# A chunked recurrence on TensorE: chunk matrices in 128x128 blocks, or as 64 columns with 64x64 quarter tiles

## What is computed

```python
def step(S, inp):
    r_t, w_t, k_t, v_t, kk_t, a_t = inp
    s_kk = jnp.einsum('bhvk,bhk->bhv', S, kk_t)
    S = (S * w_t[:, :, None, :] - s_kk[..., None] * (kk_t * a_t)[:, :, None, :]
         + v_t[..., None] * k_t[:, :, None, :])
    return S, jnp.einsum('bhvk,bhk->bhv', S, r_t)
...
_, y = lax.scan(step, S0, xs)
```

## Time and profile before

| | |
|---|---|
| device time, median of 3 runs | 1858.79 us (1856.99 to 1859.38) |
| profiled execution | its span, 1854.8 us, first to last instruction; the page gives no other time of its own |
| PE busy | 1814.8 us, 98% |
| PEld busy | 1670.1 us, 90% |
| DVE busy | 1234.7 us, 67% |
| ACT busy | 822.3 us, 44% |
| HBM traffic | 389.6 MB, 210 GB/s over the span |

### The profile page before, as it was taken

One profiled execution on the slowest core, in us unless ns is written; L12 is line 12 of the kernel. 1 busy time (PEld: TensorE's weight loads), 2 busy tenths in 40 slices (PEclk: granted clock), 3 DMA queues, 4 the chain that ended last, 5 costly groups with the idle time before them and its releaser, 6 DMA issues.

```text
span 1854.8 us, 30243 instructions
## 1 busy us (share of the span) xinstructions
PE 1814.8 (98%) x12578; PEld 1670.1 (90%) x12578; DVE 1234.7 (67%) x1826; ACT 822.3 (44%) x1106; POOL 0.2 (0%) x4
## 2 busy tenths in 40 slices
PE   9999999899999999999999999999999999999999
PEld 8889888788887779999978899999999997889999
DVE  3894455777888787876657468776876547555543
ACT  2335443543676674434443244344534444334442
POOL 0000000000000000000000000000000000000000
PEclk9999999999999999999999999999999999999999
DMA  8334310888798886786430058775785341044451
GB/s 320 136 137 159 137 69 25 329 316 305 302 359 329 337 343 256 310 332 255 165 111 24 23 217 341 301 323 229 293 320 226 159 159 46 4 157 157 164 202 69
DMA packets 65224, 391.62 MB, mean 211 GB/s; under 512 B 7360, under 2 KB 7488, under 8 KB 27328
## 3 DMA queue, kind: packets, MB, share of 16 engines
q1 hardware_dynamic: 64800, 389.61, 54.3%
q10 hardware_dynamic: 288, 0.08, 0.0%
HBM read 388.61 MB, written 1.05 MB: 210 GB/s over the span
## 4 chain that ended last, share of the span: by engine, by line
PE 88%; DVE 8%; ACT 2%; issue 1%; DVEq 0%; ACTq 0%
PE bank L501 87%; DVE region L2213 1%; PE bank L542 1%; DVE slab_low L1892 1%; DVE region L2176 0%; DVE region L1905 0%; DVE tiny L2175 0%; DVE region L2501 0%; DVE region L2478 0%; DVE region L2499 0%; DVE region L2167 0%; DVE slab_low L1973 0%; ACT region L1398 0%; DVE region L2497 0%; ACT L1328 0%
## 5 line engine op out<-in xcount | busy, mean ns | idle before, releaser
L1892 DVE TENSOR_TENSOR slab_low<-slab,w_hi 128x2048 fp32r<-128x2048 f32 x152 | 346.0, 2289 | 96.1 <-ACT w_hi L1441 95.4
L501 PE MATMUL bank<-h_hi,w_hi 128*128 128x256 f32 x1408 | 392.4, 282 | 0.0
L501 PE MATMUL bank<-h_hi,slab_low 128*128 128x256 f32 x1408 | 391.8, 281 | 0.0
L501 PE MATMUL bank<-h_lo,w_hi 128*128 128x256 f32 x1408 | 381.0, 282 | 0.0
L1441 ACT ACTIVATE w_hi<-slab 128x2048 fp32r<-128x2048 f32 x152 | 291.3, 1918 | 78.1 <-DMA slab<-in_w_ffn_in 66.6
L501 PEld LDWEIGHTS bank<-h_hi,slab_low 128*128 128x128 f32 x1408 | 270.1, 192 | 0.0
L501 PEld LDWEIGHTS bank<-h_hi,w_hi 128*128 128x128 f32 x1408 | 265.5, 189 | 0.4
L501 PEld LDWEIGHTS bank<-h_lo,w_hi 128*128 128x128 f32 x1408 | 257.8, 188 | 0.0
L501 PE MATMUL bank<-gT_hi,d_hi 128*128 128x256 f32 x832 | 234.5, 282 | 0.8 <-DVE gT_lo L2091 0.8
L501 PE MATMUL bank<-gT_lo,d_hi 128*128 128x256 f32 x832 | 234.2, 282 | 0.0
L501 PE MATMUL bank<-gT_hi,d_low 128*128 128x256 f32 x832 | 234.1, 281 | 0.0
(11 more groups left out here) (286 smaller groups left out, 2880.2 us busy)
## 6 DMA issues: line engine op xcount, KB each, us to landing
slab<-in_w_ffn_in SPq DMA_DIRECT2D x88, 1024.0 KB, 8.6
slab<-in_w_up SPq DMA_DIRECT2D x64, 1024.0 KB, 8.6
region<-in_w_ada SPq DMA_DIRECT2D x128, 512.0 KB, 6.6
region<-in_w_ffn_out SPq DMA_DIRECT2D x44, 1024.0 KB, 4.8
region<-in_w_down SPq DMA_DIRECT2D x32, 1024.0 KB, 4.8
slab<-in_w_in SPq DMA_DIRECT2D x23, 1024.0 KB, 4.8
slab<-in_w_mix_in SPq DMA_DIRECT2D x20, 1024.0 KB, 8.3
hT<-in_w_ada SPq DMA_DIRECT2D x16, 512.0 KB, 4.3
```

The source lines that it names most:

```text
L501: return nc.tensor.matmul(o, lhsT, rhs, start=start, stop=True, skip_group_check=True)
L1892: V_.tensor_tensor(slab_low[slot][:, :], slab[slot][:, :], w_hi[h % 3][:, :].bitcast(F), ALU.subtract)\
```

## The change

In words, part by part:

- The chunk matrices keep only their diagonal blocks: the 128 partitions hold the rows of two chunks, and the columns are the 64 tokens of a chunk. A group is now 256 columns (`CB`) instead of 512, and both groups lie side by side. The masks `strict`, `incl` and `level0` to `level5` become 64 columns wide, and `eyes`, two identities on top of one another, is new.
- The products of chunk matrices (`chunk_products`, `coupling`, and those of a chunk with `rows`) become matmuls of 64 rows, 64 weight columns and 64 moving columns. `chunk_products` alternates between partitions 0 to 63 and 64 to 127, both into one bank; `coupling` asks for two banks first and goes through the four combinations of contraction half and output half.
- The transposes of TT become products with `eyes`.
- Tm and TT of a group lie next to each other (`inverse`), their two products go into the two halves of one bank, and DVE subtracts both with one instruction. DVE masks the next `off` once for both groups (`level_blocks`), into one of two buffers, ahead of the updates. Levels 2 on wait for `tt_ready` of their group.
- Attention is shifted: a level's turn comes after its second products and coupling, and the output of group n-2 stands in level n, ahead of its scores. In a chunk the output of group 4+c4 stands ahead of the scores, and the turn of 5+c4 between the solution and the wait for `u_ready`. ACT follows.
- In a chunk, `BT` times v stands ahead of the wait for the state, and the output products are made in every chunk.

```diff
+        CB = 4 * CHUNK
+        HALVES = (slice(0, CHUNK), slice(CHUNK, P))
+        def chunks(name, g):
+            return B2[name][:, 0, g * CB:(g + 1) * CB]
+        def inverse(name, g):
+            return B2["Tm"][:, g, 0:CB] if name == "Tm" else B2["Tm"][:, g, CB:2 * CB]
...
+                        places = [product("dve") for _ in range(2)]
+                        for x in range(4):
+                            t, c = x // 2, x % 2
+                            for rows in HALVES:
+                                tok = slice(t * P + rows.start, t * P + rows.stop)
+                                for g, heads in enumerate(HALVES):
+                                    m = mm(places[g][rows, x * CHUNK:(x + 1) * CHUNK], V[left][heads, c, tok],
+                                           V[right][heads, c, tok], x == 0)
...
+                    def chunk_products(ps, left, right, at=0, first=True):
+                        for x in range(4):
+                            for rows in HALVES:
+                                X = slice(x * CHUNK, (x + 1) * CHUNK)
+                                m = mm(ps[rows, at + x * CHUNK:at + (x + 1) * CHUNK], left[rows, X],
+                                       right[rows, X] if right is not None else C("eyes")[rows, :],
+                                       first and x == 0)
...
                     for lev in range(1, 6):
+                        pe.wait_ge(S["off_ready"], w("off_ready"))
                         for g in range(2):
...
+                            pe.wait_ge(S["m1_ready" if lev == 1 else "tt_ready"],
+                                       w("m1_ready" if lev == 1 else "tt_ready"))
+                            off = V["off"][:, lev % 2, g * CB:(g + 1) * CB]
+                            chunk_products(product("act"), off, inverse("Tm", g)).then_inc(S["for_act"], 1)
+                        if lev == 1:
+                            short(SHORT_FIRST + 1)
+                        else:
+                            output(lev - 2)
                         scores(lev)
-                        turn(lev - 1)
                         for g in range(2):
                             pe.wait_ge(S["m1_ready"], w("m1_ready"))
+                            ps = product("dve")
                             if lev < 5:
...
+                                chunk_products(ps, inverse("TT", g), chunks("M1", g))
+                            chunk_products(ps, chunks("M1", g), inverse("TT", g), CB, lev == 5)\
+                                .then_inc(S["for_dve"], 1)
                         if lev in COUPLED:
                             coupling(*COUPLED[lev][1:3])
-                        output(lev - 1)
-                        if lev == 1:
-                            short(SHORT_FIRST + 1)
+                        turn(lev - 1)
...
-                        pe.wait_ge(S["state_ready"], w("state_ready"))
                         ps = product("act")
                         for h in range(4):
...
+                            mm(ps[rows, h * 64:(h + 1) * 64], chunks("BT", h % 2)[rows, X[h]],
+                               V["vt"][rows, t, h * 64:(h + 1) * 64], h == 0)
+                        pe.wait_ge(S["state_ready"], w("state_ready"))
                         for c in range(2):
...
+                            m = mm(ps[rows, c * P:(c + 1) * P], V["al"][:, c, tok], V["state"][:, c, :])
                         m.then_inc(S["for_act"], 1)
+                        output(4 + c4)
                         if 6 + c4 < len(GROUPS):
                             scores(6 + c4)
-                        if 5 + c4 < len(GROUPS):
-                            turn(5 + c4)
...
+                            m = mm(ps[rows, h * 64:(h + 1) * 64], inverse("TT", h % 2)[rows, X[h]],
+                                   V["R"][rows, h * 64:(h + 1) * 64], h == 0)
                         m.then_inc(S["for_dve"], 1)
                         if 5 + c4 < len(GROUPS):
-                            output(5 + c4)
+                            turn(5 + c4)
                         pe.wait_ge(S["u_ready"], w("u_ready"))
...
-                        if c4 % 2:
+                        for left, right in (("vt", "C2T"), ("negU", "C1T")):
                             for h in range(4):
...
+                                o = bank[7][HALVES[h % 2], (h // 2) * T + c4 * CHUNK:(h // 2) * T + (c4 + 1) * CHUNK]
+                                m = mm(o, V[left][rows, t, h * 64:(h + 1) * 64], chunks(right, h % 2)[rows, X[h]])
...
                 for lev in range(6):
                     scaled(lev)
+                    if 0 < lev < 5:
+                        level_blocks(lev + 1)
                     for g in range(2 if lev else 0):
+                        ps = take()
+                        at = 0 if lev < 5 else CB
+                        read(V_.tensor_tensor(V["Tm"][:, g, at:2 * CB], V["Tm"][:, g, at:2 * CB], ps[:, at:2 * CB],
+                                              ALU.subtract))
                         if lev < 5:
...
+                            dve.sem_inc(S["tt_ready"], 1)
```

More of the change, by code:

```diff
@@ L1151, in coupling @@
                     def coupling(left, right):
[L1153 to L1160, removed]
+                        places = [product("dve") for _ in range(2)]
[6 more added lines that the diff above has]
+                                           V[right][heads, c, tok], x == 0)
+                                    if x == 3 and rows.start:
+                                        m.then_inc(S["for_dve"], 1)
+                    def chunk_products(ps, left, right, at=0, first=True):
[5 more added lines that the diff above has]
+                                       first and x == 0)
+                        return m
                     coupling("be", "al")
@@ L1175, in _ @@
                         pe.wait_ge(S["tt_ready"], w("tt_ready"))
[L1176 to L1179, removed]
+                        chunk_products(product("act"), inverse("TT", g), None).then_inc(S["for_act"], 1)
                     pe.wait_ge(S["kdup_ready"], w("kdup_ready"))
@@ L1227, in _ @@
                     for c4 in range(T // CHUNK):
-                        t, r0 = c4 // 2, (c4 % 2) * CHUNK
+                        t, rows = c4 // 2, HALVES[c4 % 2]
+                        tok = slice(c4 * CHUNK, (c4 + 1) * CHUNK)
+                        X = [slice((2 * t + h // 2) * CHUNK, (2 * t + h // 2 + 1) * CHUNK) for h in range(4)]
                         short_half(4 + c4 // 2, c4 % 2)
@@ L1800, in _ @@
                     if 5 + c4 < len(GROUPS):
-                        output(5 + c4)
+                        turned(5 + c4)
                 act.wait_ge(S["read_by_act"], w.n["read_by_act"])
@@ L2477, in couple @@
                         ps = take()
[L2478 to L2486, removed]
-                                                  b3(C("level1"), 4), ALU.mult))
-                            dve.sem_inc(S["off_ready"], 1)
-                couple("AT", "strict")
+                        read(V_.tensor_tensor(blocks(chunks(dst, g)), blocks(ps[:, 0:CB]), b3(C(mask), 4), ALU.mult))
+                couple("AT", "strict")
+                level_blocks(0)
+                for g in range(2):
+                    link(V_.tensor_tensor(blocks(inverse("TT", g)), b3(C("eyes"), 4),
+                                          blocks(V["off"][:, 0, g * CB:(g + 1) * CB]), ALU.subtract))
+                    dve.sem_inc(S["tt_ready"], 1)
+                level_blocks(1)
                 scaled, probabilities = attention(GROUPS, V["sc"], V["pr"], 64 ** -0.5,
```

92 lines of the change are left out of this document (30 added, 62 removed).

## The result

Four runs of the changed kernel gave a median of 1848.03 us (1846.54 to 1854.23), four of the kernel before beside them 1859.09 us: a ratio of 0.9946, 95% interval 0.9934 to 0.9958. The change makes the kernel faster, by 10 us by that ratio (11 between the medians) and not by the 22 that I forecast. The profiled run is the fastest of the four; their mean granted clocks were 0.991, 0.991, 0.990 and 0.987, in the order of their times. In the profiled run the span fell from 1854.8 to 1844.8 us where the sum asked for 1832.6; its own time, 1846.54, shows that only 1.7 us lie around a span, so 2.3 of the 4.0 us that I put there were the spread of the runs. The missing 12 us are sought inside the span.

The account below looks back on a forecast made before the run. PE bounds the kernel (98% busy), with DVE also close in the levels. Inverse -14.0 and recurrence +2.9 make -11.1 us a layer, -22.2 in all; 1854.8 - 22.2 + 4.0 = 1836.6, said as 1836; range 1825 to 1855.

Parts of the forecast that it names:

- The price of a record: PE's quarter-tile matmuls: two overlap, 0.028 us a record instead of 0.112; bounds 0.014 and 0.112.
- rival 1: Quarter-tile pairs sharing a PSUM bank take turns, 0.056 us a record: 1861 us; chance 0.11.
- The levels: Levels 1 to 5 of the inverse: 35.2 us a layer against 48.9 before, -13.7.
- the longer of the two sums: Levels 2 and 3: 5.6 us by PE, 6.3 by the chain through DVE; the longer decides, rounded to 6.2.
- The chunks: The recurrence, chunks 0 to 3: +2.9 us a layer, bounds 0 and +5.
- The wait for u_ready: Chunks 0 and 1: u_ready comes 3.3 us after the last score record, PE has 2.0 us of work: +1.2 each.
- Shape changes and narrower products: Chunks: shape changes +0.7 a chunk; 64-column output products +0.45 in chunks 0 and 2, -0.6 in 1.
- The granted clock is 1.00 throughout: The edited stretch: clock read as 1.00 from the earlier profile; no time was put on a lower one.
- the last sentence of the prediction: Edited stretch: the forecast is wrong if a level stays above 8 us or the granted clock falls below 1.00.
- my sum: First record of chunk 0 to the last U product: 29.3 us before, 32.2 with the forecast +2.9.
- 2: Quarter-tile pairs take turns and the next weight load isn't hidden: 1895 us at 0.08 a record; chance 0.09.
- 3: Chunks pay more, U wait delaying state and scores; DVE's chain stretches levels 2 to 4 by 1 us each: 1850; chance 0.10.

Follow-up runs that it names:

- run 7: Run 3's kernel, with DVE masking the next level's blocks ahead of the scaled attention scores instead of behind them: 1827.74 us, ratio 0.9832.
- run 2: Run 1's kernel plus two full matmuls that nobody reads ahead of the u_ready wait in chunks 0 and 1: 1835.93 us, ratio 0.988.
- run 1: The changed kernel plus one, one, one and three full matmuls that nobody reads behind the turns of levels 1 to 4: 1846.32 us, ratio 0.9934.
- run 3: The changed kernel with attention's output in a chunk moved from ahead of the scores to behind the solution U: 1832.02 us, ratio 0.9858.
- run 4: Run 2's kernel with its fills made of pairs of 64x64x64 matmuls on the two diagonal quarters: 1837.81 us, ratio 0.9886.
- run 5: The changed kernel plus two unread full matmuls ahead of the u_ready wait in chunks 0 and 1, none in the levels: 1837.9 us, ratio 0.9882.

## Why the prediction was wrong

**The price of a record: right.** 30 ns for pairs that alternate, against 28 forecast, and 112 of a full tile. The rule on shared banks, by which rival 1 had 56 ns, is not borne out: the pairs of a chunk product write into the two halves of one bank and do not take turns. One quarter alone costs (0.68 - 0.23) / 7 = 64 ns, over the eight records of the first product of chunk 0, where I had 56; 0.23 us is the mean length of such a record, in the first line below. The couplings came out cheaper than I said: with all four quarters in use, 32 records take 0.69 us, (0.69 - 0.23) / 31 = 15 ns, which is my lower bound of 14 within one.

```profile
L516 PE MATMUL bank<-region 64*64 64x64 f32 x704 | 27.6, 227 | 6.4 <-issue 2.1 <-DVEq L2490 1.7 <-DVEq L2477 1.2
...
961.29 0.69 PE L516 MATMUL bank<-region 64*64 64x64 f32 x32 [1.21 <-DVEq L2477]
1007.03 0.68 PE L516 MATMUL bank<-region 64*64 64x64 f32 x8
```

**The levels: right,** 35.4 us against 35.2, each within 0.35. DVE decides levels 2 to 4, as the longer of the two sums said; run 7 showed that in 2 and 3 it is DVE's whole work and not a chain with gaps in it. (The sentence that a level above 8 us would disprove the forecast should have left out level 1, which was itself forecast at 8.9 and took 8.95.)

**The chunks: right in their parts, wrong in their clock.** The wait for u_ready was found and priced at +1.2 us; the profile has 1.1. Shape changes and narrower products come out in their sum, since run 2 has the whole stretch at 32.1 against 32.2; one by one they were not measured. (The terms that the prediction names for chunk 3, -0.9, +0.87 and three changes of 0.17, make 0.48 and not 0.65.) The step that failed is the one that was hardly a step: "The granted clock is 1.00 throughout" was read from the earlier trace rows, of a kernel whose PE is full in chunks 0 to 2, and carried over to a kernel in which a wait stands in just those chunks and the products around it have become shorter. A lower clock is in no rival and not among the terms put at nothing; only the last sentence of the prediction has it, as a sign that the forecast is wrong, and that sign came. I priced the wait at its own length. It cost that, and then the half clock behind it: the excess over my sum is 38.2 - 32.2 = 6.0 us in the first layer, 36.8 - 32.2 = 4.6 in the second (1576.36 to 1613.13), and in the second layer the 12 records behind the last output products took 4.51 us, against 2.83 for the same records of the first layer: 1.7 more.

```profile
1048.58 2.83 PE L516 MATMUL bank<-region,slab 128*128 128x256 f32 x12 [1.83 <-issue]
...
1616.51 4.51 PE L516 MATMUL bank<-region,slab 128*128 128x256 f32 x12 [1.83 <-issue]
```

Both stand behind the same wait of 1.83 us, and the clock fell behind one of them. 6.0 + 4.6 + 1.7 = 12.3 us, against the 12.2 that the span is above the sum. The MoE part, where the profile after shows one fall more than before, doesn't count: level 1 of the first layer starts at 971.6 in one and 971.7 in the other.

The Trainium skill, TensorE: Matmul & The Clock Gate, Part 1 (The HAM clock gate), says that the clock has two settings and goes by how busy PE has been lately. The trace agrees: the granted clock is within 0.01 of 1.00 or of 0.50 in every window whose bounds are those of a change, and each of the five falls begins inside a wait of PE or at most 1.3 us behind its end. That sentence could have warned me, and I had weighed one on banks in its place; which waits are enough, these runs don't tell.

**The rivals.** 1 and 2 fell with the price of a record. 3 named the right place and, by chance, nearly the right time (1850), for a reason that is not there: DVE's chain did not stretch the levels, and run 2 took the chunks' extra away without touching their order. The range held the time; the likeliest case's own did not (1825 to 1846).

## What to carry to other kernels

A wait that a change puts into PE's work can have two prices, its length and the clock behind it; here they were 1.1 and about 2.6 us per wait (6.0 + 4.6 over four waits). That the short products around these waits have a part in it is not shown: in the kernel before, a wait of 1.43 us in level 1 left the clock at 1.00, and so did the waits of the levels here. Work that an engine can do at any time (here the attention step's output) belongs ahead of the wait that the change creates, and where none is left, a few matmuls without use, in time in which the engine waits anyway, keep the clock and cost nothing that run 1 could measure. And the granted clock is a result of the kernel and not a given: when a change empties an engine, the windows of before don't tell the clock of after.

## What was not expected of the hardware

- Four quarters overlap almost fully, at 15 ns a record (one alone takes 64, a quarter of that is 16), and a pair in the two halves of one bank at 30. Issued one half after the other, the records still take 42 and not 64; what overlaps there is not known.
- The clock fell behind waits of 1.1 us (idle time on PE by the profile, 1.39 from the last record's start to the next), and stayed up, in the same kernel, behind one of 1.67 (1.94) in the levels. With these waits gone, falls stood at other places (level 5 in the profiled run of run 3, the tail in runs 2 to 5 and 7). Which of several waits brings it down can differ from layer to layer of one run; this was seen in run 3, and behind the chunks of the changed kernel, and was not explained.
- Full tiles and pairs of quarter tiles keep the clock up alike in the chunks when they fill the same waits (runs 2 and 4).
